# Mixer of a two-layer decoder: block order q, k, retention, gate, v, and every turned tile carried through VectorE and DRAM

## What is computed

```python
for l in range(DEPTH):                                  # DEPTH = 2
    x = x + 0.5 * swiglu(rmsnorm(x, norm_ffn1[l]), ...)  # FFN 1, D_FF = 2816
    h = rmsnorm(x, norm_mix[l])
    proj = h @ w_in[l]                                  # 1024 x 3072, six blocks of 512 columns
    dq, dk, dv, rq, rk, rv, rg = split(proj)            # 512 512 512 256 256 512 512
    # four heads, two maps each: softmax with a distance bias, causal
    probs = softmax(q0 k0^T * s + bias) - lam * softmax(q1 k1^T * s + bias)
    o_diff = head_rms(probs @ v) * g * (1 - lam_init)
    # four heads of retention: causal, decaying scores without softmax
    o_ret = silu(rg) * head_rms((rq rk^T * decay) @ rv)
    x = x + concat(o_diff, o_ret) @ w_out[l]            # 1024 x 1024
    x = x + 0.5 * swiglu(rmsnorm(x, norm_ffn2[l]), ...)  # FFN 2
return rmsnorm(x, norm_final)
```

## Time and profile before

| | |
|---|---|
| median of 3 runs | 951.33 us (951.28 to 952.41) |
| the profiled execution | 950.73 us, of which the core's span is 948.6 us |
| TensorE busy | 939.9 us, 99% |
| VectorE, ScalarE, GpSimd busy | 582.7, 457.0, 42.6 us |
| granted TensorE clock, mean | 0.999 of full |
| mixer, layer 0 and layer 1 | from about 191 and from about 658 us of the span |

### The profile page before, as it was taken

One profiled execution on the slowest core, in us unless ns is written; L12 is line 12 of the kernel. 1 busy time (PEld: TensorE's weight loads), 2 busy tenths in 40 slices (PEclk: granted clock), 3 DMA queues, 4 the chain that ended last, 5 costly groups with the idle time before them and its releaser, 6 DMA issues.

```text
span 948.6 us, 12194 instructions
## 1 busy us (share of the span) xinstructions
PE 939.9 (99%) x4329; PEld 779.0 (82%) x4329; DVE 582.7 (61%) x725; ACT 457.0 (48%) x597; POOL 42.6 (4%) x81
## 2 busy tenths in 40 slices
PE   9999999999999999999999999999999999999997
PEld 7888888888888888888888888888888888888885
DVE  6666556567666755656566555656675767565653
ACT  7544344455664444344355434443657454444432
POOL 4040000000010000000010000000002000000000
PEclk9999999999999999999999999999999999999999
DMA  8898766646363986766749776764744649676731
GB/s 281 274 293 249 243 199 244 207 154 204 126 219 102 296 276 197 245 203 236 226 140 286 226 243 198 252 211 150 240 138 178 222 155 281 221 245 206 240 143 61
DMA packets 161578, 201.81 MB, mean 213 GB/s; under 512 B 14064, under 2 KB 128800, under 8 KB 161536
## 3 DMA queue, kind: packets, MB, share of 16 engines
q1 hardware_dynamic: 122224, 173.82, 55.2%
q10 hardware_dynamic: 38992, 26.52, 9.4%
q0 software_dynamic: 320, 0.92, 0.5%
HBM read 187.06 MB, written 14.16 MB: 212 GB/s over the span
## 4 chain that ended last, share of the span: by engine, by line
PE 98%; DVE 1%; ACT 1%; POOL 0%; issue 0%; POOLq 0%; DVEq 0%
PE gu L1018 13%; PE gu L1020 13%; PE gu L1019 13%; PE acc L1020 10%; PE acc L1019 10%; PE acc L1018 10%; PE tp L1018 8%; PE tp L1020 8%; PE tp L1019 8%; PE gu L1044 1%; PE tp L1036 1%; PE tp L1212 1%; PE acc L1223 1%; PE tp L1235 1%; PE gu L1324 0%; ACT w_hi L366 0%
## 5 line engine op out<-in xcount | busy, mean ns | idle before, releaser
L686 DVE TENSOR_TENSOR w_lo<-raw,w_hi 128x2048 fp32r<-128x2048 f32 (+1 forms) x164 | 366.1, 2234 | 95.7 <-ACT w_hi L366 95.6
L366 ACT ACTIVATE w_hi<-raw 128x2048 fp32r<-128x2048 f32 (+1 forms) x164 | 306.1, 1869 | 29.2 <-DMA raw<-in_w_in_dram 11.4
L1018 PE MATMUL gu<-w_hi,xT_hi 128*128 128x512 f32 x558 | 219.3, 393 | 0.0
L1020 PE MATMUL gu<-w_hi,xT_lo 128*128 128x512 f32 x558 | 217.4, 390 | 0.0
L1019 PE MATMUL gu<-w_lo,xT_hi 128*128 128x512 f32 x558 | 217.2, 389 | 0.0
L1018 PE MATMUL acc<-w_hi,aT_hi 128*128 128x512 f32 x384 | 149.9, 390 | 0.0
L1020 PE MATMUL acc<-w_hi,aT_lo 128*128 128x512 f32 x384 | 149.5, 389 | 0.0
L1019 PE MATMUL acc<-w_lo,aT_hi 128*128 128x512 f32 x384 | 149.4, 389 | 0.0
L1018 PE MATMUL tp<-w_hi,xT_hi 128*128 128x512 f32 x320 | 124.7, 390 | 0.2 <-DVE w_lo L686 0.2
L1019 PE MATMUL tp<-w_lo,xT_hi 128*128 128x512 f32 x320 | 124.5, 389 | 0.0
L1020 PE MATMUL tp<-w_hi,xT_lo 128*128 128x512 f32 x320 | 124.5, 389 | 0.0
(11 more groups left out here) (164 smaller groups left out, 650.5 us busy)
## 6 DMA issues: line engine op xcount, KB each, us to landing
raw<-in_w_down_dram SPq DMA_DIRECT2D x88, 512.0 KB, 4.1
raw<-in_w_gate_dram SPq DMA_DIRECT2D x84, 512.0 KB, 4.1
raw<-in_w_up_dram SPq DMA_DIRECT2D x84, 512.0 KB, 5.3
raw<-in_w_in_dram SPq DMA_DIRECT2D x40, 512.0 KB, 5.0
bounce<-kT ACTq DMA_DIRECT2D x40, 256.0 KB, 3.9
qT<-bounce ACTq DMA_DIRECT2D x160, 64.0 KB, 2.2
raw<-in_w_out_dram SPq DMA_DIRECT2D x16, 512.0 KB, 3.7
raw<-in_w_in_dram SPq DMA_DIRECT2D x16, 256.0 KB, 3.2
```

Of the source, the lines that this page charges most:

```text
L366: nc.scalar.activation(w_hi[:, pos % SLOTS, 0:n], raw[:, pos % RAW, 0:n], ACT.Copy).then_inc(hi_done, 1)
L686: nc.vector.tensor_tensor(w_lo[:, pos % SLOTS, 0:n], raw[:, pos % RAW, 0:n], w_hi[:, pos % SLOTS, 0:n].bitcast(F32), ALU.subtract).then_in ...
L1018: nc.tensor.matmul(out_, s_hi, m_hi, start=first, stop=False)
L1020: return nc.tensor.matmul(out_, s_lo, m_hi, start=False, stop=last)
```

## The change

The blocks come in another order (`BLOCK_COLS`): q, k, r, then v of retention, gate, v of attention; the retention half of `w_out` comes before the attention half (`OUT_ROWS`). All 24 transposes of k, r and softmax results leave TensorE in each layer. In their place `to_blocks` turns both halves of q, k and r, and each pair of halves makes the trip to DRAM and back: two sends of 256 KB, one `fetch` of four 128 KB DMAs. `probs_to_blocks` turns each head's softmax results on VectorE; `send_probs` and `fetch_probs` carry two heads at a time (384 KB out, four DMAs of 96 KB back) to the new tile `probs_back`, from which ScalarE copies them (`read_probsT`). The score, norm and output steps are the same instructions at other places.

The diff, cut to what is spoken of below:

```diff
+BLOCK_COLS = (0, 1, 3, 4, 5, 2)
+OUT_ROWS = (2, 3, 0, 1)
...
+                def send_probs(pair):
+                    act.wait_ge(probs_blocked, 4 * layer + 2 * pair + 2)
+                    act.dma_start(probs_bounce[pair, ...], probs_blocks(pair)...).then_inc(p_out, 16)
+
+                def fetch_probs(pair):
+                    act.wait_ge(p_out, 16 * (2 * layer + pair + 1))
...
                 read_proj(1, 0, dq_dk[:, 0, 512:1024])
                 prep(6)
+                send(2, k_out)
                 read_proj(1, 1, dq_dk[:, 1, 512:1024])
-                fetch_q()
+                act.wait_ge(q_out, 32 * (layer + 1))
+                fetch(0, gate[:, :, :].rearrange("p t n -> p (t n)"), q_in)
                 prep(7)
-                read_proj(2, 0, dv[:, 0, :])
+                send(3, k_out)
+                read_proj(2, 0, rqk[:, 0, :])
                 prep(8)
-                read_proj(2, 1, dv[:, 1, :])
+                send(4, r_out[0])
+                act.wait_ge(k_out, 32 * (layer + 1))
+                fetch(2, hid, k_in)
+                read_proj(2, 1, rqk[:, 1, :])
...
+                read_probsT(2)
+                read_probsT(3)
+                read_proj(5, 1, dv[:, 1, :])
+                for tt in range(TT):
+                    act.wait_ge(ro_rstd_done, 2 * layer + tt + 1)
+                    act.wait_ge(pv_ready, 2 * layer + tt + 1)
+                    head_squares(tt, gu[tt], o_sq_done)
                 prep(16)
                 prep(17)
...
 VectorE:
+                to_blocks(3, 4, dq_dk[:, 1, 512:1024])
                 prep(7)
-                read_qkT(0, 0, kT[:, :, 0:P])
+                to_blocks(4, 5, rqk[:, 0, :])
                 for tt in range(TT):
                     turned(tt, q_in, qT[:, :, tt * P:(tt + 1) * P], q_turned)
-                read_qkT(1, 1, kT[:, :, P:SEQ])
                 prep(8)
+                to_blocks(5, 6, rqk[:, 1, :])
+                for tt in range(TT):
+                    turned(2 + tt, k_in, kT[:, :, tt * P:(tt + 1) * P], k_turned)
+                prep(9)
                 biased_max(0)
...
+                prep(10, PIECE // 2)
+                for h in (0, 1):
+                    probs(h)
+                    probs_to_blocks(h)
                 for h in (2, 3):
-                    dve.wait_ge(probsT_psum, HEADS * layer + h - 1)
                     biased_max(h)
+                for tt in range(TT):
+                    turned(4 + tt, r_in, rT[:, :, tt * P:(tt + 1) * P], r_turned)
...
+                prep(15)
                 prep(16)
+                for pair in range(2):
+                    diff_norm(pair, gu[pair])
...
 TensorE:
+                for c in (1, 2):
+                    block_of(c, 0)
+                    block_of(c, 1)
+                block_of(3, 0)
                 pe.wait_ge(q_turned, 2 * layer + 2)
-                pe.wait_ge(qkT_done, 3 * layer + 2)
+                pe.wait_ge(k_turned, 2 * layer + 2)
                 scores(0)
                 scores(1)
-                block_of(3, 0)
                 block_of(3, 1)
-                transpose_probs(0)
-                transpose_probs(1)
                 for h in (2, 3):
                     pe.wait_ge(negmax_done, HEADS * layer + h - 1)
                     scores(h)
                 block_of(4, 0)
...
+                pe.wait_ge(r_turned, 2 * layer + 2)
...
+                block_of(5, 1, ro_T)
+                pe.wait_ge(mT_lo_done, 4 * layer + 1)
+                add_rows(layer, 0, 0, MIX0 + W0, aT_hi, aT_lo, 0, first=True)
+                pe.wait_ge(proj_read, n_read + 12)
+                for pair in range(2):
+                    pe.wait_ge(probsT_done, HEADS * layer + 2 * pair + 2)
+                    diff_out(pair, gu[pair])
+                pe.wait_ge(mT_lo_done, 4 * layer + 2)
+                add_rows(layer, 0, 1, MIX0 + W0, aT_hi, aT_lo, 0, first=True)
+                add_rows(layer, 0, 0, MIX0 + W0 + 1, aT_hi, aT_lo, 2)
+                diff_T(0)
+                add_rows(layer, 0, 1, MIX0 + W0 + 1, aT_hi, aT_lo, 2, hook=lambda: diff_T(1))
```

More of the change, by code:

```diff
@@ L257, in _ @@
                         load(layer, 0, MIX0 + 2 * c + h, srcs, kk * 512)
-                for w in range(4):
-                    load(layer, 0, MIX0 + W0 + w, [w_out[layer, (2 * w + k) * P:(2 * w + k + 1) * P, :] for k in range(2)])
+                for i, w in enumerate(OUT_ROWS):
+                    load(layer, 0, MIX0 + W0 + i, [w_out[layer, (2 * w + k) * P:(2 * w + k + 1) * P, :] for k in range(2)])
                 ffn(layer, FFN2, w2_gate, w2_up, w2_down)
@@ L550, in send, with fetch @@
                 def send(n, done):
-                    act.wait_ge(qr_blocks, 3 * layer + n + 1)
+                    act.wait_ge(turned_blocks, 6 * layer + n + 1)
                     act.dma_start(turn_bounce[n, :, :, :].rearrange("p q n -> p (q n)"),
                                   turn_blocks(n).rearrange("p q i n -> p (q i n)")).then_inc(done, 16)
-                def fetch_q():
-                    act.wait_ge(q_out, 32 * (layer + 1))
+                def fetch(n, back, done):
                     for q in range(4):
[L558 to L565, removed]
+                        act.dma_start(back[32 * q:32 * q + 32, :].rearrange("c (b n) -> c b n", n=P),
+                                      turn_bounce[n:n + 2, :, q, :].rearrange("t (b c) n -> c (t b) n", b=4)).then_inc(done, 16)
                 act.wait_ge(rstd_done, TT * (3 * layer + 1) + TT)
@@ L586, in mixer @@
                 nc.scalar.activation(lam_exp[:, own], lam_dot[:, own], ACT.Exp).then_inc(lam_exped, 1)
+                prep(10, PIECE // 2)
                 for tt in range(TT):
[L588 to L592, removed]
+                    act.wait_ge(r_out[tt], 16 * (layer + 1))
+                act.wait_ge(k_turned, 2 * (layer + 1))
+                fetch(4, hid, r_in)
+                exps(0)
+                exps(1)
+                read_proj(3, 1, rv[:, 1, :])
+                prep(11, PIECE // 2)
+                send_probs(0)
+                prep(12, PIECE // 2)
+                exps(2)
+                exps(3)
+                fetch_probs(0)
+                read_proj(4, 0, gate[:, 0, :], ACT.Silu)
+                read_proj(4, 1, gate[:, 1, :], ACT.Silu)
+                prep(13, PIECE // 2)
                 read_probsT(0)
@@ L620, in mixer @@
                 mixed_hi(2, xT_hi[:, 4:8, 0:P], tp[0])
-                ahead(layer, FFN2)
+                ahead(layer, FFN2, [0])
                 mixed_hi(3, xT_hi[:, 4:8, P:SEQ], tp[1])
+                ahead(layer, FFN2, [1])
             for i, norm in enumerate((norm_ffn1, norm_mix, norm_ffn2)):
@@ L1106, in project, with add_rows @@
                     ins.then_inc(ready, 1)
-            def add_rows(layer, it, tt, pos, src_hi, src_lo, k0, first=False, last=False):
+            def add_rows(layer, it, tt, pos, src_hi, src_lo, k0, first=False, last=False, hook=None):
                 if tt == 0:
@@ L1114, in add_rows @@
                 for half in range(2):
+                    if hook and half:
+                        hook()
                     for k in range(2):
@@ L1225, in scores @@
                     ins.then_inc(scores_ready, 1)
-                def transpose_probs(h):
-                    pe.wait_ge(probs_done, 2 * (HEADS * layer + h) + 2)
-                    transposes(tp[h % 2], [z(h, 0, i * P, (i + 1) * P) for i in range(3)], probsT_psum)
                 def causal(dst, done):
```

158 lines of the change are left out of this document (68 added, 90 removed).

## The result

| | before | changed |
|---|---|---|
| median of 4 runs | 951.87 us (951.28 to 952.48) | 960.23 us (959.42 to 963.36) |
| ratio, 95% interval | | 1.0095 [1.0082, 1.0107] |
| profiled execution | 950.73 us, span 948.6 | 959.42 us, span 957.6 |
| granted TensorE clock, mean | 0.999 | 0.995 |

The direction was forecast (955.0, slower), the size was not: 960.2 lies above the range that ended at 959.0. The profiled executions differ by 8.7 us, their spans by 9.0. The changed kernel is slower by 0.95% (0.82 to 1.07%). The other three executions of it took 959.7, 960.7 and 963.4 us, at mean clocks of 0.995, 0.993 and 0.992.

What follows compares the result with a forecast made beforehand. TensorE, busy 99% of the span, was taken to bound the kernel. Terms -5.3 + 4.9 + 0.2 + 4.0 = +3.8 us on the 951.33 median gave 955.1, forecast as 955.0, range 949.8 to 959.0.

Steps and rivals of the forecast that it cites:

- Transposes: 24 transposes a layer leave TensorE, all on the path: 2.64 us a layer, 5.3 us saved in all.
- Term A: TensorE waits before the first scores for k's trip through DRAM: 1.8 us in layer 0, 3.1 in layer 1, together 4.9.
- Term B: Trip of r and softmax results, before the retention scores: VectorE just about makes it, 0.1 us a layer, 0.2 in all.
- Term C: TensorE waits for the attention norm before diff_T(0), behind piece 16's parts: 2.0 us in both layers, 4.0 in all.
- The clock: Granted TensorE clock stays at full speed throughout, no term in the sum; a gap long enough to lower it was only a caveat.
- K's trip: Rival: send and fetch of k take 4 us each, wait before the scores 0 to 0.5; 950.4 us, chance 0.24.
- the trips are slow: Rival: DMA trips slower than forecast, Term A 8 to 11, Term B 1 to 2; 958 to 963 us, chance 0.15.
- the first rival: K's trip is hidden before the first scores: send 4 us, fetch 4; 950.4 us, chance 0.24.
- a send would land early: Rule beside the row: with DMA queues taking turns, ScalarE's send passes SP's loads, giving the first rival's sum.

Runs made afterwards that it cites:

- e7: Kernel before the change, with each of the 24 transposes a layer that the change removes done twice on TensorE; 956.89 us, ratio 1.0061.
- e3: Changed kernel with the load of piece 9 held on SyncE until the fetch of k has landed; 962.86 us, ratio 1.0106.
- e4: Changed kernel with both e1's norm move and e3's held load of piece 9; 956.44 us, ratio 1.0042.
- e6: e4 with parts of pieces 9 and 10 made later, behind exponentials (ScalarE) and first two heads' softmax results (VectorE); 949.50 us, ratio 0.9977.
- e1: Changed kernel with both attention norms ahead of the low part of piece 16 on VectorE; 953.31 us, ratio 1.0014.
- e9: Changed kernel with 17 identity transposes on TensorE right ahead of its wait for the attention norm; 961.13 us, ratio 1.0098.
- e10: e9 with 24 more identity transposes ahead of the wait for k before the first scores; 955.97 us, ratio 1.0054.
- e2: Changed kernel with k turned by TensorE again, the rest still through DRAM; 953.65 us, ratio 1.0025.
- e5: Changed kernel with both e1's norm move and e2's k turned by TensorE; 948.17 us, ratio 0.9971.
- e8: e6 with VectorE's low part of piece 10 moved behind the copies into rT; 949.54 us, ratio 0.9978.

## Why the forecast was off, step by step

- **Transposes, -5.3.** Right: e7 gives 5.6 for as many. The distance between entries of the chain was the right price.
- **Term A, 4.9.** Right in mechanism and place, too small: 6.1. The send took 7.4 and 7.3 us for 7 taken, which is little. The larger error was the fetch. I took its landing from the median of q's fetch (5.2) where it took 6.1 and 5.9, and 1.8 for its issue where it took 2.7 in layer 0 and 2.0 in layer 1. e3 shows that the landing is long because of the loads (2.8 us for the same fetch); why one issue was held is not shown. Layer 0 has the larger wait, not layer 1 as forecast: the issue was slower there, and in layer 1 TensorE came to the scores 12.9 us after the send and not 11.5.
- **Term B, 0.2.** Right, zero. That it was close is shown by e3, e4 and e6, where a delay on VectorE makes this the wait.
- **Term C, 4.0.** Right to a tenth of a microsecond, and e1 shows the chain.
- **The clock.** The step that failed. "The granted clock stays at full speed, and nothing in the sum depends on it" was carried over from a kernel in which TensorE hardly stops. The forecast itself made four gaps of 1.8 to 3.1 us, and kept the clock for its last paragraph as something that would make it wrong. It should have been a term: 1.7 us for each gap behind which it falls, two in the profiled execution, 3.4 us. How many fall could not have been read from the trace before, so the range had to hold none to four, 0 to 6.8 us. With the true size of A and without this term the sum would be -5.6 + 6.1 + 4.0 = +4.5, 955.8 us, inside the range; with it +7.9, 959.2 us, just outside.
- **The rivals.** K's trip was not hidden. That the trips are slow is half true: the fetch was slower than taken, but A was 6.1 and not 8 to 11, and B was 0. The median, 960.2, lies within that rival's 958 to 963 by luck: the clock brought it there, not the trips. The send did not take the 4 us of the first rival but 7.4 beside loads, and 5.3 with the later loads held (e3). The Trainium skill, DMA: Bandwidth & Descriptors, section Queues, rings and completion order, says that each DMA engine takes turns between the queues that it has work for. No run here shows such turns, or their absence; that a send would land early by them did not come true.
- **Open.** Why a gap brings half clock in one execution and not in the next was not settled. Nor what makes e9's other executions longer: the medians of e9 and e10 differ by 5.2 us, where the 48 further transposes (5.6 us) take the place of as much idle time and two stretches of half clock are 3.4. Nor why one of e10's five executions took 959.6 us at a clock of 0.996: only its first was traced.

## What to carry to other kernels

A gap on a TensorE that was always busy costs its length and the half clock that it may bring behind it (here 2.0 us of idle cost up to 3.7), so both belong in the sum, and the second is seen only in the granted clock right behind the gap, since it counts as busy time. Look first at what stands ahead of the awaited instruction on its own engine: one line on VectorE was worth 6.9 us here, more than all 48 transposes. Where a wait can't be removed, empty work in front of it can pay: 4.3 us with both gaps of a layer filled (e10). With only the gap before the norm filled the median did not fall (961.1 for 960.2, e9).

## What the runs showed of the hardware

- After gaps of 1.7 to 2.7 us the granted clock fell to 0.50, the 1.2 GHz level, for 3.4 us each time: eleven times in the traces of the changed kernel, e2, e3, e4 and e9, 1.7 us lost each. It did not fall after five gaps of 2.6 to 3.4 us before the first scores (changed kernel, e1, e9). The changed kernel, with four such gaps, had a mean clock of 0.992 to 0.995 in all four executions. The kernels whose largest gap in the mixers is 1.3 us or less (the kernel before, e5 to e8) had 0.998 or more in every one.
- With 17 transposes of the identity in the place of the idle time, the granted clock behind it was 1.00 (e10), where it was 0.69 and 0.50 without them.
- A fetch of 128 KB in rows of 128 numbers (512 bytes) landed 6.1 us after its issue beside weight loads and 2.8 us with the next loads held back; a send of 256 KB after 7.4 and 5.3 us (layer 0, changed kernel and e3).
- A transpose of 128x128 in a row of others cost TensorE 0.116 us (e7).
